# State space input matrices turned by VectorE blocks and DMA; fourth u lot one K tile later; last h_lo tiles ahead of the last u tiles

## The chip, the core and the metric

The kernel runs on one core of a Trainium2 chip. The metric is the device time of one launch in microseconds (us), the median of several runs; lower is better. The engines named here are TensorE (PE; its weight loads are PEld), VectorE (DVE), ScalarE (ACT), GpSimd (POOL) and SyncE (SP). SP computes nothing: it issues all DMAs of the kernel, in the order of its program, to one hardware queue that the core's 16 DMA engines serve.

## What is computed

The reference is a decoder trunk of two layers, for 512 tokens of 1024 channels in float32. Only the state space (S5) branch of the mixing part is touched by the change. There are 32 groups of 16 channels with 64 complex states each.

```
for l in range(DEPTH):                                   # DEPTH = 2
    x = x + 0.5 * swiglu(rms_norm(x, ffn1_norm[l]), ffn1_w1[l], ffn1_w3[l], ffn1_w2[l])
    h = rms_norm(x, mix_norm[l])
    p = h @ w_in[l]
    p_m2, p_s5, p_dsa, p_hg = jnp.split(p, IN_SPLITS, axis=-1)
    y_b = s5_branch(p_s5, ...)                           # beside mamba2, dsa and hgrn2 branches
    ...                                                  # gated merge, w_out
    x = x + 0.5 * swiglu(rms_norm(x, ffn2_norm[l]), ffn2_w1[l], ffn2_w3[l], ffn2_w2[l])

def s5_branch(u, ...):
    bb_re = q_re[..., None] * b_re - q_im[..., None] * b_im
    bb_im = q_re[..., None] * b_im + q_im[..., None] * b_re
    bu_re = jnp.einsum("blgi,gpi->blgp", ug, bb_re)      # the input matrices at work
    bu_im = jnp.einsum("blgi,gpi->blgp", ug, bb_im)
    _, _, s_re, s_im = lax.associative_scan(combine, (a_re, a_im, bu_re, bu_im), axis=1)
    y = einsum(s_re, c_re) - einsum(s_im, c_im) + d_skip * u ; y = gelu(y) ; GLU
```

## The kernel before

**Lots.** Every large product is cut into lots. A lot is one weight tile of 1024 x 128 (512 KB); its product with 512 tokens fills one PSUM bank. SP loads it into one of four slots of `raw`; ACT copies it to `w_hi` (L424), DVE or POOL forms `w_lo = raw - w_hi` (L432), and PE makes three passes for each of the eight K tiles (L493 to L495: hi by hi, lo by hi, hi by lo). A slot of `raw` is loaded anew when its `w_lo` is done. The order of the lots and of all other work in the mixing part is a list of steps, `script()`, that each engine walks in the same order. PE waits for `lo_done` of the lot and for its bank at `begin`, and for `h_done` of each K tile where the activations are fresh.

**The stage of the change.** The first feed-forward part ends with eight "down" lots. The mixing part begins with `s5_w` phase 0, then `quad` of u: four lots `u0` to `u3` of the state space input, walked K tile by K tile for all four, on activations that are not normalised yet. In between PE sums the squares (L536), ACT and DVE make `rstd`, and DVE writes the normalised tiles `normed`, which ACT copies over `h_hi` and DVE over `h_lo` (L1857) as soon as `quad` is through with a tile. DVE then scales the four u outputs into `s5_uc` (`keep_u`, L1863, shown in the trace as `s_uc`) and forms `w_lo` of the next lot. After `quad` come `s5_w` phase 1, the lots `ks` and `q0`, a small transpose `turn_small` (L720), `q1`, `q2`, and `s5_in` (L760): 128 matmuls for the 32 groups, stationary operand `s5_w`, moving operand `s5_u`. Lots `q3`, `k0` and then `s5_out` follow.

**The input matrices.** POOL computes them early, during the feed-forward part, as `s5_pre` (the trace writes `s_pre`, and so for all s5 names), with the 64 states of two groups on the partitions. `s5_in` needs them turned. `s5_w` does that on PE: eight times four transposes of 128x128 (L748) in two phases of 16 each, with eight copies from PSUM by ACT (L1531).

**SP's order in this stage**, all in one queue: `s5_taps` out to DRAM (8 DMAs, L1165), the lots up to `k`'s first ones, eight DMAs that load `s5_t` from `s5_taps` (L1171; 256 KB each, into 16 partitions each), four that store `s5_uc` to `s5_ud` in DRAM (L1177; 256 KB each, from 128 partitions, each after its `keep_u`), and, when all four have landed, two lots and eight DMAs that load `s5_u` (L1184; 128 KB each, into 16 partitions each). `s5_in` on PE waits for all eight of `s5_u`.

Of the kernel before, what the change touches and what calls it, by code (L numbers as in the profile page):

```python
# [20 lines left out]
S5_W_TURNS = ((0, 1, 2, 3), (4, 5, 6, 7))  # L21
S5_W_BANK = (4, 5, 6, 7, 4, 5, 6, 7)
# [25 lines left out]
def script():  # L48
# [33 lines left out]
    s = [("s5_w", 0), ("quad", "u", 0), ("s5_w", 1)] + lots(("ks", 1)) + [("lot", "q", 0), ("turn_small",)]  # L82
# [119 lines left out]
def trunk(nc, x_in, positions, w_lots, par_in, s5_in, con_in, gamma_in, out, s5_taps, s5_ud):  # L202
# [5 lines left out]
    with ctx:  # L208
# [35 lines left out]
        def PC(name, i):  # L244
# [26 lines left out]
        s5_pre = at("s5_pre", [P, 2, 16, P], f32, A + 13)  # L271
# [14 lines left out]
        s5_w = at("s5_w", [P, 2, 16, P], f32, M)  # L286
# [69 lines left out]
            s5_aj s5_ca_ready s5_mag_ready s5_gen s5_tap_psum s5_tap_done s5_tap_d s5_tap_out s5_w_psum s5_w_done  # L356
# [112 lines left out]
        def _(pe):  # L469
# [200 lines left out]
            def quad(kind, i):  # L670
# [66 lines left out]
            def s5_w_(phase):  # L737

                if phase == 0:
                    pe.wait_ge(S["s5_gen"], 1)  # L740
                for j in S5_W_TURNS[phase]:
                    if j == 6:

                        pe.wait_ge(S["rstd_ready"], R(2))
                    if j >= 4:
                        pe.wait_ge(S["s5_w_done"], j - 3)
                    for i in range(4):
                        m = pe.transpose(bank[S5_W_BANK[j]][:, P * i:P * (i + 1)], s5_pre[:, j // 4, 4 * (j % 4) + i],  # L748
                                         ident)
                    m.then_inc(S["s5_w_psum"], 1)  # L750
# [314 lines left out]
            def hg_end(h):  # L1065
# [4 lines left out]
                         quad=quad, s5_w=s5_w_, s5_in=s5_in_, s5_out=s5_out, s5_back=s5_back,  # L1070
# [25 lines left out]
        def _(sp):  # L1096
# [29 lines left out]
            for layer in range(DEPTH):  # L1126
# [171 lines left out]
        def _(act):  # L1298
# [146 lines left out]
            def lot(kind, i):  # L1445
# [9 lines left out]
                elif kind in ("q", "k"):  # L1455
                    evac(da_qk[:, 4 * "qk".index(kind) + i], n)
# [1135 lines left out]
```

## Time and profile before

| | |
|---|---|
| median of 3 runs | 2833.62 us (2833.0 to 2834.78) |
| profiled execution, from first to last instruction | 2830.9 us |
| PE busy | 2819.4 us of it |
| DVE, ACT, POOL busy | 1591.8, 1193.4, 708.1 us |
| DMA | 275.72 MB, mean 97 GB/s |
| instructions | 38776 |

The profiled execution's only own time is its span, 2830.9 us; it leaves out what lies before the first and behind the last instruction, and the median of the runs is 2.7 us more. An edit is priced in the span and the same number of microseconds is added to the median.

How to read it: PE is busy practically all the time, so a microsecond is won only where PE has less to do or waits less, and it is lost where PE begins to wait. Matmuls are pipelined, so the distance between the starts of two PE rows, not the length that a row states, is what a pass costs. The views used are the page's first part, the timeline of an engine (a row is a start, a length and what ran), the view of DMA issues with the time from issue to landing, and the view of stretches with the DMA rate in each.

### The profile page before, as it was taken

To read this page: it belongs to the slowest core of one execution; us is meant where nothing else is said; L and a number is where in the kernel's file an instruction comes from. 1 tells how busy PE (TensorE), PEld (TensorE's weight loads), DVE (VectorE), ACT (ScalarE), POOL (GpSimd) and SP (SyncE) were. 2 spreads that over 40 slices of the span, in tenths; PEclk is the share of its full clock that TensorE was granted. 3 is DMA by queue.
4 is the path that set the end of the run, shared out by engine and by line. 5 is a ranking of instruction groups with operands and counts; after the bars stand their busy time and mean duration, and the time that the engine had idled before them with its cause. 6 is when DMAs were issued, how large, how long until landed. Compare 5 with 4: busy or idle time off the path is not lost.

```text
span 2830.9 us, 38776 instructions
## 1 busy us (share of the span) xinstructions
PE 2819.4 (100%) x14364; PEld 2305.9 (81%) x14364; DVE 1591.8 (56%) x2312; ACT 1193.4 (42%) x1732; POOL 708.1 (25%) x336
## 2 busy tenths in 40 slices
PE   9999999999999999999999999999999999999999
PEld 7888888877788888888888888888777888888887
DVE  5575557685657454343544845576846673543433
ACT  5343354556355344222343423445553653442222
POOL 0075014333334440000000840234333344300000
PEclk9999999999999999999999999999999999999999
DMA  5333394222222233333333333932222223233332
GB/s 188 97 96 97 99 147 120 82 75 67 82 82 83 90 97 98 97 96 97 96 127 97 94 97 113 151 97 83 74 75 82 83 82 90 90 103 97 97 97 82
DMA packets 95601, 275.72 MB, mean 97 GB/s; under 512 B 17648, under 2 KB 30832, under 8 KB 94960
## 3 DMA queue, kind: packets, MB, share of 16 engines
q1 hardware_dynamic: 95472, 273.95, 34.2%
q8 instruction: 87, 1.43, 0.2%
q14 instruction: 42, 0.34, 0.0%
HBM read 264.48 MB, written 5.24 MB: 95 GB/s over the span
## 4 chain that ended last, share of the span: by engine, by line
PE 97%; DVE 2%; DMA 0%; ACT 0%; issue 0%; SPq 0%; ACTq 0%; DVEq 0%
PE bank L493 29%; PE bank L495 29%; PE bank L494 29%; PE bank L521 1%; PE bank L523 1%; PE bank L522 1%; PE bank L852 1%; PE bank L871 1%; PE bank L886 1%; PE bank L985 1%; PE bank L826 0%; DVE h_lo L1857 0%; PE bank L1043 0%; DVE s_uc L1863 0%; PE bank L1055 0%; PE bank L760 0%
## 5 line engine op out<-in xcount | busy, mean ns | idle before, releaser
L493 PE MATMUL bank<-h_hi,w_hi 128*128 128x512 f32 x2512 | 989.5, 394 | 2.4 <-DVE h_lo L1857 2.3
L495 PE MATMUL bank<-h_hi,w_lo 128*128 128x512 f32 x2512 | 978.1, 389 | 0.0
L494 PE MATMUL bank<-h_lo,w_hi 128*128 128x512 f32 x2512 | 977.8, 389 | 0.0
L424 ACT ACTIVATE w_hi<-raw 128x1024 fp32r<-128x1024 f32 x482 | 508.0, 1058 | 897.8 <-PE bank L495 881.5
L432 POOL TENSOR_TENSOR w_lo<-raw,w_hi 128x1024 fp32r<-128x1024 f32 x208 | 521.3, 2511 | 1090.5 <-ACT w_hi L424 1090.5
L493 PEld LDWEIGHTS bank<-h_hi,w_hi 128*128 128x128 f32 x2512 | 471.6, 188 | 108.2 <-issue 8.3
L495 PEld LDWEIGHTS bank<-h_hi,w_lo 128*128 128x128 f32 x2512 | 471.6, 188 | 99.2
L494 PEld LDWEIGHTS bank<-h_lo,w_hi 128*128 128x128 f32 x2512 | 471.8, 188 | 96.9 <-issue 1.9
L432 DVE TENSOR_TENSOR w_lo<-raw,w_hi 128x1024 fp32r<-128x1024 f32 x274 | 361.8, 1321 | 271.2 <-ACT w_hi L424 271.0
L493 PE MATMUL bank<-g_hi,w_hi 128*128 128x512 f32 x698 | 272.5, 390 | 0.0
L495 PE MATMUL bank<-g_hi,w_lo 128*128 128x512 f32 x698 | 271.6, 389 | 0.0
L494 PE MATMUL bank<-g_lo,w_hi 128*128 128x512 f32 x698 | 271.6, 389 | 0.0
L1892 DVE TENSOR_TENSOR gated<-bank,rstd 128x512 f32<-128x512 f32 x88 | 60.8, 691 | 217.0 <-PE bank L495 217.0
L1243 POOL TENSOR_TENSOR s_mag<-s_k,con 128x1024 f32<-128x1024 f32 x2 | 3.8, 1908 | 661.2 <-DVE s_k L2044 661.2
L1889 DVE TENSOR_TENSOR silu_a<-bank,rstd 128x512 f32<-128x512 f32 x88 | 60.7, 690 | 168.8 <-PE bank L495 147.3
L493 PEld LDWEIGHTS bank<-g_hi,w_hi 128*128 128x128 f32 x698 | 131.0, 188 | 28.4 <-DVE g_lo L1898 1.4
L495 PEld LDWEIGHTS bank<-g_hi,w_lo 128*128 128x128 f32 x698 | 131.0, 188 | 27.2
L494 PEld LDWEIGHTS bank<-g_lo,w_hi 128*128 128x128 f32 x698 | 131.1, 188 | 27.0
L493 PE MATMUL bank<-y_hi,w_hi 128*128 128x512 f32 x256 | 101.5, 396 | 0.0
L495 PE MATMUL bank<-y_hi,w_lo 128*128 128x512 f32 x256 | 99.8, 390 | 0.0
L494 PE MATMUL bank<-y_lo,w_hi 128*128 128x512 f32 x256 | 99.7, 389 | 0.0
L1502 ACT ACTIVATE gate_th<-bank 128x512 f32<-128x512 f32 x64 | 38.0, 594 | 140.4 <-PE bank L495 140.3
(374 smaller groups left out, 3336.9 us busy)
## 6 DMA issues: line engine op xcount, KB each, us to landing
raw<-in_w_lots SPq DMA_DIRECT2D x482, 512.0 KB, 3.6
s_t<-s_taps SPq DMA_DIRECT2D x16, 256.0 KB, 14.1
da_s<-da_qk SPq DMA_DIRECT2D x16, 256.0 KB, 4.1
x_nat<-in_x SPq DMA_DIRECT2D x4, 512.0 KB, 7.5
s_ud<-s_uc SPq DMA_DIRECT2D x8, 256.0 KB, 4.4
s_u<-s_ud SPq DMA_DIRECT2D x16, 128.0 KB, 8.8
s_bc<-in_s SPq DMA_DIRECT2D x2, 512.0 KB, 5.6
s_bp<-in_s SPq DMA_DIRECT2D x2, 512.0 KB, 6.6
```

The costliest lines, as they stand in the source:

```text
L424: act.activation(w_hi[:, s], raw[:, s], AFT.Copy).then_inc(S["hi_done"], 1)
L432: eng.tensor_tensor(w_lo[:, s], raw[:, s], w_hi[:, s].bitcast(f32), SUB).then_inc(S["lo_done"], 1)
L493: pe.matmul(b[:, :], w_hi[:, s, kw], xh[:, k], start=(k == 0), stop=False)
L494: pe.matmul(b[:, :], w_hi[:, s, kw], xl[:, k], start=False, stop=False)
L495: return pe.matmul(b[:, :], w_lo[:, s, kw], xh[:, k], start=False, stop=(k == nk - 1))
L521: pe.matmul(o, h_hi[:, k, tok], wh[:, :, k], start=(k == 0), stop=False)
L522: pe.matmul(o, h_lo[:, k, tok], wh[:, :, k], start=False, stop=False)
L523: m = pe.matmul(o, h_hi[:, k, tok], wl[:, :, k], start=False, stop=(k == KT - 1))
L852: m = pe.matmul(logit_bank(u, e)[:, 0:P * (b + 1)], da_qk[r, hp, P * b:P * (b + 1)], da_qk[r, 4 + hp, 0:P * (b + 1)], start=True, stop=True)
L1502: act.activation(gate_th[:, i % 2], bank[t % 4][:, :], AFT.Tanh, scale=0.5).then_inc(S["free%d" % (t % 4)], 1)
L1889: V.tensor_tensor(silu_a[:, q], bank[ta % 4][:, :], rstd[:, :], MUL).then_inc(S["free%d" % (ta % 4)], 1)
L1892: V.tensor_tensor(gated[:, q], bank[tb % 4][:, :], rstd[:, :], MUL).then_inc(S["free%d" % (tb % 4)], 1)
```

## The change

1. `s5_w` is taken out of the script on PE and ACT: 32 transposes and eight copies a layer, and the waits for them.
2. POOL writes the same numbers into `s5_pre` in another layout, in 24 instructions of 512 elements as before; the innermost elements that it writes now lie 64 bytes apart.
3. DVE turns `s5_pre` in place in blocks of 32x32 with two instructions, behind the down lots of the second third of the feed-forward part, and waits for `s5_gen` (POOL's end) before them.
4. SP stores the result to a new DRAM buffer `s5_wd` (2 DMAs of 1 MB, ahead of `s5_taps`) and loads it from there into `s5_w` (8 DMAs of 256 KB, into 32 partitions each) right behind the eight of `s5_t` and ahead of the four of `s5_uc`.
5. `s5_in` waits for these eight instead of ACT's copies, and reads `s5_w` with a distance of 64 bytes between neighbouring columns.
6. In `quad` the lot `u3` begins with K tile 1, and does its tiles 0 and 1 there; the first `h_step` is given there.
7. DVE writes the last two `h_lo` tiles before `keep_u(2)` and `keep_u(3)`, not after them.
8. ACT waits for `s5_w_out` before it writes `q0`'s output, which lies over `s5_pre`.

On SP, the place in layer 0 behind the first feed-forward part, before:

```order
L1134 DMA raw<-in_w_lots 128x1024
L1130 REGISTER_ALU
L1130 COMPARE_AND_BRANCH
L1171 DMA s_t<-s_taps 16x32x128 x8
L1177 DMA s_ud<-s_uc 128x512 x4
L1102 DMA raw<-in_w_lots 128x1024
L1184 DMA s_u<-s_ud 16x32x64 x4
L1102 DMA raw<-in_w_lots 128x1024
L1184 DMA s_u<-s_ud 16x32x64 x4
```

The same place of the changed kernel:

```order
L1118 DMA raw<-in_w_lots 128x1024
L1114 REGISTER_ALU
L1114 COMPARE_AND_BRANCH
L1158 DMA s_t<-s_taps 16x32x128 x8
L1164 DMA s_w<-s_wd 32x4x512 x8
L1169 DMA s_ud<-s_uc 128x512 x4
L1086 DMA raw<-in_w_lots 128x1024
L1176 DMA s_u<-s_ud 16x32x64 x4
L1086 DMA raw<-in_w_lots 128x1024
L1176 DMA s_u<-s_ud 16x32x64 x4
```

Eight DMAs, 2 MB in all, stand between `s5_t` and the stores of `s5_uc`; the rest keeps its order.

On DVE, the end of `quad` in layer 0, before:

```order
L1868 SCALAR_TENSOR_TENSOR normed<-x,par,rstd 128x512
L1863 TENSOR_TENSOR s_uc<-bank,rstd 128x512 x2
L432 TENSOR_TENSOR w_lo<-raw,w_hi 128x1024
L1863 TENSOR_TENSOR s_uc<-bank,rstd 128x512 x2
L1857 TENSOR_TENSOR h_lo<-normed,h_hi 128x512 x2
```

The same place of the changed kernel:

```order
L1856 SCALAR_TENSOR_TENSOR normed<-x,par,rstd 128x512
L1851 TENSOR_TENSOR s_uc<-bank,rstd 128x512 x2
L430 TENSOR_TENSOR w_lo<-raw,w_hi 128x1024
L1845 TENSOR_TENSOR h_lo<-normed,h_hi 128x512 x2
L1851 TENSOR_TENSOR s_uc<-bank,rstd 128x512 x2
```

The last two tiles of `h_lo` have changed places with the last two of `s5_uc`.

The diff, cut to its core:

```diff
-    s = [("s5_w", 0), ("quad", "u", 0), ("s5_w", 1)] + lots(("ks", 1)) + [("lot", "q", 0), ("turn_small",)]
+    s = [("quad", "u", 0)] + lots(("ks", 1)) + [("lot", "q", 0), ("turn_small",)]
...
-        s5_pre = at("s5_pre", [P, 2, 16, P], f32, A + 13)
+        s5_pre = at("s5_pre", [P, 2, 4, 32, S5_TILES], f32, A + 13)
...
-        s5_w = at("s5_w", [P, 2, 16, P], f32, M)
+        s5_w = at("s5_w", [P, 2, P, S5_TILES], f32, M)
...
                 for k in range(KT - 2):
                     pe.wait_ge(S["h_done"], H(H_RAW[1] + k + 1))
-                    for j in range(4):
+                    for j in range(4 if k else 3):
                         if k == 0:
                             begin(n0 + j, 0, OUT[n0] + j)
+                        if (k, j) == (1, 3):
+                            begin(n0 + 3, 0, OUT[n0] + 3)
+                            part(3, 0).then_inc(S["h_step"], 1)
                         m = part(j, k)
-                    m.then_inc(S["h_step"], 1)
+                    if k:
+                        m.then_inc(S["h_step"], 1)
...
             def s5_in_():
                 pe.wait_ge(S["s5_u_in"], 16 * S5_Q)
-                pe.wait_ge(S["s5_w_done"], 8)
+                pe.wait_ge(S["s5_w_in"], 16 * 8)
...
-                                          s5_w[:, c, st, 64 * e:64 * e + 64], s5_u[:, 2 * st + e], start=True, stop=True)
+                                          s5_w[:, c, 64 * e:64 * e + 64, st], s5_u[:, 2 * st + e], start=True, stop=True)
...
                 ring(3, MIX0 // 4)
+                for i in range(2):
+                    sp.wait_ge(S["s5_w_turned"], i + 1)
+                    sp.dma_start(s5_wd[i], s5_pre[:, i].rearrange("p b q a -> p b (q a)")).then_inc(S["s5_w_out"], 16)
                 sp.wait_ge(S["s5_tap_d"], 4)
...
+                sp.wait_ge(S["s5_w_out"], 32)
+                for i in range(2):
+                    blocks = s5_wd[i].rearrange("(a r) b x -> b r a x", a=4)
+                    for b in range(4):
+                        sp.dma_start(s5_w[32 * b:32 * b + 32, i].rearrange("r (a q) t -> r a (q t)", a=4), blocks[b]).then_inc(S["s5_w_in"], 16)
                 turn = FFN2_0 // 4 + 3
...
-                for t in range(4):
-                    r = slice(4 * t, 4 * t + 4)
-                    shape = [P, 4, S5_Q, 16]
-                    ar, an = (s5_pw[:, i, r, S5_Q + 1:S5_POW].unsqueeze(3).broadcast_to(shape) for i in (1, 4))
-                    bre, bim = (s5_bb[:, i, r].unsqueeze(2).broadcast_to(shape) for i in range(2))
-                    pre = [s5_pre[:, i, r].rearrange("p a (s i) -> p a s i", i=16) for i in range(2)]
+                for b in range(4):
+                    shape = [P, 16, 2, 16]
+                    at_ = S5_Q + 1 + 2 * b
+                    ar, an = (s5_pw[:, i, :, at_:at_ + 2].unsqueeze(3).broadcast_to(shape) for i in (1, 4))
+                    bre, bim = (s5_bb[:, i].unsqueeze(2).broadcast_to(shape) for i in range(2))
+                    pre = [s5_pre[:, i, b].rearrange("p (s i) a -> p a s i", s=2) for i in range(2)]
...
+                    if (kind, i) == ("q", 0):
+                        act.wait_ge(S["s5_w_out"], 32)
...
                 split_lo(V, MIX0 + 4)
+                rest(KT - 2)
+                rest(KT - 1)
                 keep_u(2)
                 keep_u(3)
-                rest(KT - 2)
-                rest(KT - 1)
...
+                elif phase == 3:
+                    V.wait_ge(S["s5_gen"], 1)
+                    for i in range(2):
+                        both = s5_pre[:, i].rearrange("p b q a -> p b a q")
+                        V.transpose(both, both).then_inc(S["s5_w_turned"], 1)
```

## Rows read from the trace of the kernel before

**Rows 1.** The page, its first line and the first line of busy times.

```profile
span 2830.9 us, 38776 instructions
PE 2819.4 (100%) x14364; PEld 2305.9 (81%) x14364; DVE 1591.8 (56%) x2312; ACT 1193.4 (42%) x1732; POOL 708.1 (25%) x336
```

**Rows 2.** Timeline of PE: start us, length us, what, [idle before and releaser]; both layers.

```profile
374.98 1.91 PE L748 MATMUL bank<-con,s_pre 128*128 128x128 f32 x16
376.64 0.48 PE L493 MATMUL bank<-h_hi,w_hi 128*128 128x512 f32 x1
...
378.78 0.39 PE L493 MATMUL bank<-h_hi,w_hi 128*128 128x512 f32 x1
...
399.38 1.91 PE L748 MATMUL bank<-con,s_pre 128*128 128x128 f32 x16
...
407.21 0.50 PE L493 MATMUL bank<-h_hi,w_hi 128*128 128x512 f32 x1 [1.15 <-DVE h_lo L1857]
...
425.00 3.95 PE L760 MATMUL bank<-s_u,s_w 128*64 128x64 f32 x128
...
1830.60 3.95 PE L760 MATMUL bank<-s_u,s_w 128*64 128x64 f32 x128
```

**Rows 3.** Timeline of SP: when single DMAs of layers 0 and 1 were issued.

```profile
387.19 2.29 SPq L1171 DMA_DIRECT2D s_t<-s_taps  x1
...
401.65 0.32 SPq L1177 DMA_DIRECT2D s_ud<-s_uc  x1
...
412.96 1.25 SPq L1184 DMA_DIRECT2D s_u<-s_ud  x1
...
1817.46 1.31 SPq L1184 DMA_DIRECT2D s_u<-s_ud  x1
```

**Rows 4.** DMA issues: KB each, us from issue to landing, of those four DMAs.

```profile
s_t<-s_taps SPq DMA_DIRECT2D x1, 256.0 KB, 16.2
...
s_ud<-s_uc SPq DMA_DIRECT2D x1, 256.0 KB, 4.0
...
s_u<-s_ud SPq DMA_DIRECT2D x1, 128.0 KB, 10.2
...
s_u<-s_ud SPq DMA_DIRECT2D x1, 128.0 KB, 11.1
```

**Rows 5.** Stretches: PE, PEld, DVE, ACT, POOL busy, PE clock, DMA share, GB/s.

```profile
383.00:397.00 14.00, 14.00 (x63) 11.57 (x62) 10.39 (x15) 7.47 (x10) 0.00 (x0) 1.00 1.28 102
423.00:427.00 4.00, 4.00 (x78) 3.38 (x78) 0.00 (x0) 2.49 (x3) 1.59 (x1) 1.00 1.01 404
485.00:491.00 6.00, 5.99 (x28) 4.50 (x28) 5.46 (x7) 2.23 (x6) 2.27 (x1) 1.00 0.90 208
...
2830.00:2831.00 1.00, 0.00 (x0) 0.00 (x0) 0.00 (x0) 0.00 (x0) 0.00 (x0) 0.54 0.00 0
```

**Rows 6.** Timelines of DVE and ACT about the start of mixing, layer 0.

```profile
376.27 1.23 DVE L432 TENSOR_TENSOR w_lo<-raw,w_hi 128x1024 fp32r<-128x1024 f32 x1 [0.40 <-ACT w_hi L424]
...
398.33 1.21 DVE L432 TENSOR_TENSOR w_lo<-raw,w_hi 128x1024 fp32r<-128x1024 f32 x1
399.46 2.16 DVE L1863 TENSOR_TENSOR s_uc<-bank,rstd 128x512 f32<-128x512 f32 x2
401.52 5.63 DVE L1857 TENSOR_TENSOR h_lo<-normed,h_hi 128x512 fp32r<-128x512 f32 x2
...
398.95 1.32 ACT L1524 ACTIVATE h_hi<-normed 128x512 fp32r<-128x512 f32 x2 [2.40 <-PE bank L495]
```

**Rows 7.** Timelines of POOL, DVE and ACT, earlier in layer 0.

```profile
254.69 0.53 POOL L1265 MEMSET s_tap<- 128x512 f32 x1
...
282.45 0.69 DVE L1889 TENSOR_TENSOR silu_a<-bank,rstd 128x512 f32<-128x512 f32 x1 [4.70 <-PE bank L495]
...
362.93 1.06 ACT L424 ACTIVATE w_hi<-raw 128x1024 fp32r<-128x1024 f32 x1 [1.89 <-PE bank L495]
```

**Rows 8.** Timeline of PE: its last instructions of the span.

```profile
2827.40 0.44 PE L654 MATMUL bank<-con,x 128*128 128x128 f32 x2 [0.30 <-DVE x L1923]
```

More of the change, by code:

```diff
@@ L20 @@
 S5_POW = 2 * S5_Q + 1
-S5_W_TURNS = ((0, 1, 2, 3), (4, 5, 6, 7))
-S5_W_BANK = (4, 5, 6, 7, 4, 5, 6, 7)
 PI = math.pi
@@ L199, with trunk @@
 CON_OFF = 97 * TILE + 96
-def trunk(nc, x_in, positions, w_lots, par_in, s5_in, con_in, gamma_in, out, s5_taps, s5_ud):
+def trunk(nc, x_in, positions, w_lots, par_in, s5_in, con_in, gamma_in, out, s5_taps, s5_ud, s5_wd):
     f32, f32r, i32, u32 = mybir.dt.float32, mybir.dt.float32r, mybir.dt.int32, mybir.dt.uint32
@@ L355, in trunk @@
         MIXED = """normed_ready h_step mg_hi_done mg_done s5_in s5_step s5_args s5_powers s5_phase s5_rot
-            s5_aj s5_ca_ready s5_mag_ready s5_gen s5_tap_psum s5_tap_done s5_tap_d s5_tap_out s5_w_psum s5_w_done
+            s5_aj s5_ca_ready s5_mag_ready s5_gen s5_tap_psum s5_tap_done s5_tap_d s5_tap_out s5_w_turned s5_w_out s5_w_in
             s5_u_out s5_u_in s5_bu s5_bu_used s5_state s5_taps_in s5_y s5_y2_act s5_y2_dve s5_back s5_y_used m2_zs
@@ L532, in norm_sums @@
                 pe.wait_ge(S["sq_used"], KT * (R(r) + 1))
-                if r == 1:
-                    pe.wait_ge(S["s5_w_done"], len(S5_W_TURNS[0]))
                 pe.matmul(bank[6][:, :], ones, sq_sum[:, :], start=True, stop=True).then_inc(S["sq_sums"], 1)
@@ L735, in branch @@
                     gemm(n, 0, y_hi, y_lo, BT, k0=BT * half, t0=OUT[n] + half, ready=None if half else ready)
[L737 to L750, printed above, removed]
             def s5_in_():
                 pe.wait_ge(S["s5_u_in"], 16 * S5_Q)
-                pe.wait_ge(S["s5_w_done"], 8)
+                pe.wait_ge(S["s5_w_in"], 16 * 8)
                 pe.wait_ge(S["small_done"], 1)
@@ L1069, in _ @@
                          gate=gate, branch=branch, merge=merge, da_square=da_square,
-                         quad=quad, s5_w=s5_w_, s5_in=s5_in_, s5_out=s5_out, s5_back=s5_back,
+                         quad=quad, s5_in=s5_in_, s5_out=s5_out, s5_back=s5_back,
                          s5_end=s5_end, da_norm=da_norm, da_rope=da_rope, da_index=da_index, da_topk=da_topk, att_start=att_start,
@@ L1526, in quad @@
                     split_hi(act, n + 4 + j)
-            def s5_w_(phase):
-                for j in S5_W_TURNS[phase]:
-                    act.wait_ge(S["s5_w_psum"], j + 1)
-                    act.activation(s5_w[:, j // 4, 4 * (j % 4):4 * (j % 4) + 4].rearrange("p a b -> p (a b)"),
-                                   bank[S5_W_BANK[j]][:, :], AFT.Copy).then_inc(S["s5_w_done"], 1)
             def s5_in_():
@@ L1777, in _ @@
                          gate=gate, branch=branch, merge=merge, da_square=da_square,
-                         quad=quad, s5_w=s5_w_, s5_in=s5_in_, s5_out=s5_out, s5_back=s5_back,
+                         quad=quad, s5_in=s5_in_, s5_out=s5_out, s5_back=s5_back,
                          s5_end=s5_end, da_norm=da_norm, da_rope=da_rope, da_index=da_index, da_topk=da_topk, att_start=att_start,
@@ L2053, in quad @@
                 normalise_h()
-            def s5_w_(phase):
-                pass
             def s5_in_():
@@ L2400, in _ @@
                          gate=gate, branch=branch, merge=merge, da_square=da_square,
-                         quad=quad, s5_w=s5_w_, s5_in=s5_in_, s5_out=s5_out, s5_back=s5_back,
+                         quad=quad, s5_in=s5_in_, s5_out=s5_out, s5_back=s5_back,
                          s5_end=s5_end, da_norm=da_norm, da_rope=da_rope, da_index=da_index, da_topk=da_topk, att_start=att_start,
@@ L2588 @@
     args.append(nc.dram_tensor("s5_ud", (BW, S5_Q, S5_CH), _mybir.dt.float32, kind="Internal").ap())
+    args.append(nc.dram_tensor("s5_wd", (2, P, 4, 16 * 32), _mybir.dt.float32, kind="Internal").ap())
     trunk(nc, *args)
```

## Prediction

> **What bounds the kernel now.** Read the page's busy times first: PE is busy 2819.4 us of a span of 2830.9 us [rows 1]. Whatever takes work from PE can help, up to the next thing that PE then meets. So the second view is PE's timeline about the start of mixing, where the change lies. PE comes from the down lots, does 16 transposes from 374.98 to 376.64 (1.66 us), runs `quad`, does 16 more from 399.38, walks `ks` and has to wait 1.15 us for the last `h_lo` until 407.21, and reaches `s5_in` at 425.00 (layer 1: 1830.60) with no wait shown [rows 2]. The third view is what `s5_in` needs: the eight loads of `s5_u`. The last was issued at 412.96 and took 10.2 us to land, so it landed at 423.2; in layer 1, 1817.46 + 11.1 = 1828.6 [rows 3, 4]. PE came 1.8 and 2.0 us later than that. This is the whole slack of the DMA chain, and it is the number that decides here: the chain is as long as PE's own path, less two microseconds.
>
> Follow that chain back. The last `s5_t` load, issued at 387.19, landed at 403.4; the last store of `s5_uc`, issued at 401.65, landed at 405.7 [rows 3, 4]; only then does SP issue the `s5_u` loads. Between 383 and 397 us the DMA engines show a share of 1.28 at only 102 GB/s [rows 5]: they work through the `s5_t` loads, without a gap, in the order of issue. A load that waited 16.2 us to land when its siblings take 2.6 us each (256 KB at 102 GB/s) had a queue before it.
>
> **Part 1, PE work that goes.** Two phases of 16 transposes: 2 x 1.66 = 3.3 us a layer. The wait of 1.15 us for `h_lo` goes too, see part 2. Where `quad` starts earlier, `u3` would meet its `w_lo`: DVE forms it from 376.27 to 377.50 [rows 6]; three K tiles of the other lots take 378.78 - 376.64 = 2.14 us [rows 2], so `u3` would have begun at 377.1, and in the new order it begins at about 379.2. No wait. ACT's eight copies go as well, and ACT is not what PE waits for. PE alone would reach `s5_in` 4.2 to 4.5 us earlier a layer: `ks` will wait some 0.3 us for its `w_lo`, since that ended at 399.54 [rows 6] and moves forward with `quad` by 1.66 us to 397.9, while PE is through with `quad` at 399.38 - 1.66 = 397.7. So PE arrives at about 425.00 - 4.2 = 420.8.
>
> **Part 2, DVE's order.** The two `h_lo` tiles took 5.63 us, from 401.52, at the end of the chain [rows 6]. Now they stand before `keep_u(2)`, right behind ACT's `h_hi` (398.95 + 1.32 - 1.66 = 398.6 at the end), and end by 400 even at 0.7 us each. `keep_u(2)` and `(3)` took 2.16 us and ended at 401.62 [rows 6]; behind the two tiles they end near 401.5. So the stores of `s5_uc` can be issued no earlier than before: the gain in PE's path does not come to the DMA chain.
>
> **Part 3, the eight new loads.** They are issued behind `s5_t` and ahead of the stores of `s5_uc`, in the same queue, 8 x 256 KB = 2.1 MB. SP issues them early (before 397 it waits for `keep_u` anyway), but the engines are held by `s5_t` until 403.4, so they run after it. Their price is the rate. Loads into 16 partitions ran at 102 GB/s, the stretch 485 to 491, in which four copies into 32 partitions each ran, shows 208, and lots into 128 partitions 404 [rows 5]. The new loads go into 32 partitions each: 2.1 MB / 208 GB/s = 10.1 us. The bounds are 5.2 us (404) and 20.6 us (102); I take 10.1, since that row has the same count of partitions. So the four stores land about 10.1 us later, SP issues the `s5_u` loads 10.1 us later, and the last lands at 423.2 + 10.1 = 433.3. `s5_in` begins there instead of at 425.0: 8.3 us later. In layer 1 it is 1828.6 + 10.1 - 1830.6 = 8.1 us. PE waits 433.3 - 420.8 = 12.5 us. All of parts 1 and 2 is inside this wait: 4.2 us a layer saved in front of a later join are worth nothing.
>
> The Trainium skill, "SBUF — State Buffer", section on the DMA port swizzle, says that a transfer's rate follows the ports that its partitions reach: 16 partitions about 109 GB/s, 32 about 218, all 128 up to 436. By that figure the eight loads would be an estimated 9.6 us instead of 10.1. The trace agrees, with 102, 208 and 404 GB/s [rows 5].
>
> **Part 4, `s5_in` itself.** It takes 3.9 us now [rows 2]. Two things can lengthen it. After 12 us of idling PE's clock will be down: at the end of the span PE's last row begins at 2827.40, and in 2830 to 2831 the granted clock reads 0.54 [rows 8, 5]; half of 2.4 GHz is its lower level. A stage run wholly at that level would take 3.9 us more, one run wholly at the upper level nothing. And the stationary operand is now read at a distance of 64 bytes; no row shows such a read, nothing excludes that it costs nothing, and I bound it by 0 and another 3.9 us (each read twice as slow). Neither can be a gain, since the same 128 matmuls run at a clock and from a layout that are at best as good as before. Of 0 to 7.8 us I take 2.0 a layer, half a doubling, since the clock comes back while the stage runs.
>
> The same page, in its note on SBUF lines, says that consecutive accesses should fall in the same 16-byte line, and that each new line costs. Every column of `s5_w` is such a new line, so by that rule the strided read would cost, an estimate of up to one more doubling; no run here shows it yet.
>
> **Part 5, what is hidden.** DVE's two turns: 2048 elements a partition each, at 1.21 us for 1024 [rows 6] about 2.4 us each, 4.8 in all. DVE idled 4.70 us at just that place, until 282.45 [rows 7], and nobody waits for that `silu_a` within the next lots. Its new wait for POOL: POOL was done at 255.2, DVE gets there at 277.75; 22 us for 24 instructions, so each may be 0.9 us longer for its strided writes. If it were more, all of DVE's `w_lo` would queue behind that wait. The stores to `s5_wd`: 2.1 MB at 404 GB/s, 5.2 us in the queue, issued near 346, ahead of `s5_taps` and the lot whose `w_hi` ACT starts at 362.93 on a release by PE [rows 7]; four slots of `raw` cover it. ACT's wait for `s5_w_out` is long over.
>
> **Sum.** 8.3 + 8.1 + 2 x 2.0 = 20.4 us. The span goes from 2830.9 to 2851.3, the median of the runs from 2833.6 to 2854.
>
> **Rivals.**
> *Fast loads.* The new loads run at 404 GB/s, since they come from DRAM in pieces of 2 KB and the copies in that 208 GB/s row are between partitions. Then 5.2 us: 423.2 + 5.2 - 425.0 = 3.4, layer 1 3.2, with the clock at 1 each: 8.6, so 2842. For it: that source differs. Against it: the 16-partition loads come from DRAM too, and were at a quarter.
> *Strided weights are dear.* Rate as forecast, `s5_in` doubled twice over: 16.4 + 2 x 7.8 = 32, so 2866.
> *Not slower.* The queue is not serial: while `s5_t` holds only the ports of 16 partitions, packets of the new loads slip beside it, and they are in before 403. Then the `s5_u` loads land at 423.2 as before, PE arrives at 420.8 and waits 2.4 us: gains 1.8 + 2.0 = 3.8 us, so 2829.8. The point from which it decides is that slack: the new loads may cost the chain less than 1.8 us. For it: 102 GB/s is a quarter of what the engines can move. Against it: a store issued at 401.65 landed in 4.0 us, only after the last `s5_t` at 403.4, and a share of 1.28 leaves no engine free. To gain all of PE's 4.2 us a layer (2825) the `s5_uc` stores would have to come earlier, and `keep_u` does not let them.
>
> **Chances.** The forecast 0.60 (2848 to 2860), fast loads 0.13, strided weights 0.12, not slower 0.14 of which 0.03 faster by more than 0.2%, the rest 0.01. A difference of 0.2%, 5.7 us, is about what measuring this kernel can tell from no change. Faster 0.03, same 0.11, slower 0.86. The range runs from fast loads without any clock loss (2840) to the dear weights (2866).
>
> **What would show it.** In the profile of the changed kernel: no transposes of `s_pre` on PE; a wait of about 12 us of PE before `s5_in` in each layer, released by a DMA (`s_u`); `s_w` loads landing between 403 and 414 and `s_ud` behind them; no wait for `h_lo` in `ks`; a granted clock under 1 behind the stall. A PE wait under 3 us before `s5_in`, or `s_ud` landing at 406, would prove the queue argument wrong; a wait of 7 us, the rate; an `s5_in` of over 8 us, the weight read.

## The result, and the profile after

| | us |
|---|---|
| before, median of 5 runs (range) | 2833.78 (2833.0 to 2834.78) |
| after, median of 5 runs (range) | 2858.65 (2855.89 to 2860.54) |
| difference of the medians | +24.9 |
| ratio, with its 95% interval | 1.0088 [1.0077, 1.0099] |
| profiled execution, span: before, after | 2830.9, 2854.1 (+23.2) |

The forecast was 2854 us, in a range of 2840 to 2866. The changed kernel is slower, by somewhat more than forecast. The profiled execution of after is the quickest of its five (2855.89), and in it 23.2 of the 24.9 us can be followed.

The first view is the page of after: the first line, the busy times, and from the part on the chain the shares by engine.

```profile
span 2854.1 us, 38652 instructions
PE 2820.1 (99%) x14300; PEld 2306.7 (81%) x14300; DVE 1597.4 (56%) x2316; ACT 1185.3 (42%) x1716; POOL 712.2 (25%) x336
...
PE 95%; DMA 2%; DVE 1%; SPq 1%; ACT 0%; issue 0%; ACTq 0%; DVEq 0%
```

Against [rows 1], PE has 64 instructions fewer and is 0.7 us longer busy, though 6.6 us of transposes went. So some other work on PE became dearer, and the rest of the 23 us is time in which PE does nothing. The list of PE's waits, which gives the idle time in all, the count and the longest, has one large entry:

```profile
PE bank L744 <- DMA s_u<-s_ud: 25.2, 2, 13.6
```

Line 744 is `s5_in`, which begins only when a DMA into `s_u` has landed. PE's timeline in both layers (start, length, idle before and releaser) shows where these 25.2 us are, and what came behind them:

```profile
375.27 0.39 PE L491 MATMUL bank<-h_hi,w_hi 128*128 128x512 f32 x1
...
432.33 7.41 PE L744 MATMUL bank<-s_u,s_w 128*64 128x64 f32 x128 [11.56 <-DMA s_u<-s_ud]
439.66 0.50 PE L491 MATMUL bank<-h_hi,w_hi 128*128 128x512 f32 x1
...
1850.44 7.55 PE L744 MATMUL bank<-s_u,s_w 128*64 128x64 f32 x128 [13.64 <-DMA s_u<-s_ud]
1857.92 0.50 PE L491 MATMUL bank<-h_hi,w_hi 128*128 128x512 f32 x1
```

The same place in the kernel before, the first matmul behind `s5_in` in each layer:

```profile
428.88 0.50 PE L493 MATMUL bank<-h_hi,w_hi 128*128 128x512 f32 x1
...
1834.48 0.50 PE L493 MATMUL bank<-h_hi,w_hi 128*128 128x512 f32 x1
```

With [rows 2] this gives the whole account. After's down lots end 0.29 us later (375.27 against 374.98), which is taken off in the first layer.

| term | layer 0 | layer 1 | sum |
|---|---|---|---|
| `s5_in` begins later | 432.33 - 425.00 - 0.29 = 7.0 | (1850.44 - 1830.60) - (439.66 - 428.88) = 9.1 | 16.1 |
| `s5_in` itself is longer, to the first matmul behind it | (439.66 - 432.33) - (428.88 - 425.00) = 3.45 | (1857.92 - 1850.44) - (1834.48 - 1830.60) = 3.6 | 7.05 |
| sum | 10.5 | 12.7 | 23.2 |

The sum is the difference of the spans. PE arrives at `s5_in` at 432.33 - 11.56 = 420.8 us: the gain of parts 1 and 2 is there, and lies whole inside the wait.

The queue is seen in SP's timeline (when a DMA was issued) and, for the same DMAs in the same order, in the list of issues (us from issue to landing). They are the last `s_t`, the last `s_w`, the last `s_ud` and the last `s_u` of layer 0:

```profile
387.78 2.41 SPq L1158 DMA_DIRECT2D s_t<-s_taps  x1
397.00 0.56 SPq L1164 DMA_DIRECT2D s_w<-s_wd  x1
401.75 0.77 SPq L1169 DMA_DIRECT2D s_ud<-s_uc  x1
422.06 1.23 SPq L1176 DMA_DIRECT2D s_u<-s_ud  x1
```

```profile
s_t<-s_taps SPq DMA_DIRECT2D x1, 256.0 KB, 14.9
...
s_w<-s_wd SPq DMA_DIRECT2D x1, 256.0 KB, 15.2
...
s_ud<-s_uc SPq DMA_DIRECT2D x1, 256.0 KB, 12.9
...
s_u<-s_ud SPq DMA_DIRECT2D x1, 128.0 KB, 10.2
```

Landings: 402.7, 412.2, 414.6, 432.3. The eight new loads are the 9.5 us between the first two; 2.1 MB in that time are 221 GB/s. The last store of `s5_uc` was issued at the same time as before [rows 3] but took 12.9 us instead of 4.0 [rows 4], since it stood behind them. PE begins `s5_in` at the very moment of the last landing.

### The profile page after: what moved, and what is told of

Same layout as the page of the kernel before. It is cut to its first block, busy times and chain, and to the rows that moved or that the text cites. A ratio compares the mean times of both kernels' runs of the same rounds, so it can differ in the third digit from the quotient of the medians.

```text
span 2854.1 us, 38652 instructions
## 1 busy us (share of the span) xinstructions
PE 2820.1 (99%) x14300; PEld 2306.7 (81%) x14300; DVE 1597.4 (56%) x2316; ACT 1185.3 (42%) x1716; POOL 712.2 (25%) x336
## 4 chain that ended last, share of the span: by engine, by line
PE 95%; DMA 2%; DVE 1%; SPq 1%; ACT 0%; issue 0%; ACTq 0%; DVEq 0%
PE bank L491 28%; PE bank L493 28%; PE bank L492 28%; PE bank L519 1%; PE bank L521 1%; PE bank L520 1%; DMA s_ud<-s_uc 1%; PE bank L836 1%; PE bank L855 1%; PE bank L870 1%; DMA s_u<-s_ud 1%; PE bank L969 1%; PE bank L744 1%; PE bank L810 0%; SPq L1176 0%; PE bank L1027 0%
```

## Experiments

Every ratio is against the kernel before, run beside it on the same chip; there before had medians of 2833.1 to 2833.2. Two theories of the 23 us stood against each other at first. The queue: the new loads hold the DMA engines for their own 9 to 10 us, so without them `s5_in` begins on time. Its rival: the loads slip beside the `s5_t` loads, and it is something else that delays the `s5_u` burst. A second question was the longer `s5_in`: the low clock behind the wait, or the read at 64 bytes' distance.

### The eight loads away

After, in which the eight loads are left out and DVE fills `s5_w` with zeros.

```diff
-                for i in range(2):
-                    blocks = s5_wd[i].rearrange("(a r) b x -> b r a x", a=4)
-                    for b in range(4):
-                        sp.dma_start(s5_w[32 * b:32 * b + 32, i].rearrange("r (a q) t -> r a (q t)", a=4), blocks[b]).then_inc(S["s5_w_in"], 16)
...
+                V.memset(s5_w[:, :, :, :].rearrange("p c q t -> p (c q t)"), 0.0).then_inc(S["s5_w_in"], 1)
```

> The changed kernel without its eight loads of s5_w; VectorE sets s5_w to zero at the start of mixing instead, in time in which it idles, so s5_in works on zeros (part of the computation is left out). Theory (one serial queue): s_ud lands at about 405.7 again, the last s_u at about 423.4, PE waits some 2.3 us before s5_in in each layer instead of 11.6 and 13.6. s5_in still reads with a distance of 64 bytes and takes 6.4 us at the upper clock. Time 2833.8 - 3.8 + 2 x 2.5 = 2835. Rival (the loads slip beside s5_t, and the time went elsewhere, into GpSimd's layout or VectorE's turns): PE still waits over 8 us, 2850 to 2859.

Measured: 2839.67 us, ratio 1.0021 [1.0012, 1.003]. PE's timeline at `s5_in`, both layers:

```profile
425.31 7.64 PE L744 MATMUL bank<-s_u,s_w 128*64 128x64 f32 x128 [4.76 <-DMA s_u<-s_ud]
...
1831.89 7.67 PE L744 MATMUL bank<-s_u,s_w 128*64 128x64 f32 x128 [2.11 <-DMA s_u<-s_ud]
```

The time above before falls from 24.9 us to 6.5, and `s5_in` of layer 0 begins at 425.31, 0.3 us from where it began before. The waits of 11.56 and 13.64 us have become 4.76 and 2.11. The rival is refuted. `s5_in` itself stays 3.7 us longer in each layer, where the expectation had 2.5. The wait of layer 0 is longer than expected too: the last `s_u` landed at 425.3 where [rows 3, 4] give 423.2 for before. The last `s_t` had landed 1.2 us later and the last `s_ud` 1.4 us later, although the same DMAs stood right ahead of them. Why is not shown; in the runs here whose eight `s5_t` loads go first, the last of them landed anywhere from 402.1 to 404.7. Both are why the time came out above the expectation.

### Only the strided read

Before, with nothing changed but the layout of `s5_w`: ACT's copies write it so that the stationary operand is read at a distance of 64 bytes, as in after.

```diff
-        s5_w = at("s5_w", [P, 2, 16, P], f32, M)
+        s5_w = at("s5_w", [P, 2, P, S5_TILES], f32, M)
...
-                                          s5_w[:, c, st, 64 * e:64 * e + 64], s5_u[:, 2 * st + e], start=True, stop=True)
+                                          s5_w[:, c, 64 * e:64 * e + 64, st], s5_u[:, 2 * st + e], start=True, stop=True)
```

> The kernel before, with s5_w laid out as in the changed kernel: ScalarE's eight copies write at a distance of 64 bytes and s5_in reads so. PE does not stall and its clock is at the upper level. Theory A (the strided read costs 50 ns a matmul where a packed one costs 30): s5_in 6.4 us, time 2833.8 + 2 x 2.5 = 2838.8. Theory B (only the clock): s5_in 3.9 us, 2833.8. ScalarE's copies may be longer, which is hidden either way.

Measured: 2840.81 us, ratio 1.0025 [1.0015, 1.0036]. PE's timeline at `s5_in`, and the stretch within the first (columns as in [rows 5]: the third from the end is the granted clock):

```profile
425.71 7.39 PE L760 MATMUL bank<-s_u,s_w 128*64 128x64 f32 x128
...
1835.04 7.45 PE L760 MATMUL bank<-s_u,s_w 128*64 128x64 f32 x128 [0.25 <-DMA s_u<-s_ud]
```

```profile
427.00:429.00 2.00, 2.00 (x40) 2.00 (x40) 0.00 (x0) 1.56 (x3) 1.79 (x1) 1.00 0.94 375
```

No stall, a clock of 1.00, and still 7.4 us instead of 3.95: 58 ns a matmul instead of 31. The read costs 3.45 to 3.5 us a layer, 7 us in all, and the time rises by 7.6; `s5_in` of layer 0 also begins 0.7 us later (425.71 against 425.00). The expectation missed low.

### Only the low clock

After, in which `s5_in` reads `s5_w` as if it were packed (other columns than it should).

```diff
-                                          s5_w[:, c, 64 * e:64 * e + 64, st], s5_u[:, 2 * st + e], start=True, stop=True)
+                                          s5_w[:, c].rearrange("p q t -> p (q t)")[:, P * st + 64 * e:P * st + 64 * e + 64], s5_u[:, 2 * st + e], start=True, stop=True)
```

> The changed kernel, with s5_in reading neighbouring elements of s5_w instead of every sixteenth, at the same wait. It multiplies by the wrong columns, so the state space branch's result is not the one wanted; the amount of work is the same. Theory A (the strided read costs): s5_in falls from 7.4 us to 5.0 to 5.5, what is left above 3.9 being the clock after the stall; time 2858.7 - 4.4 = 2854. Theory B (the clock alone costs): s5_in stays at 7.4 us and the time at 2858.7.

Measured: 2853.53 us, ratio 1.0068 [1.0053, 1.0083]. PE's timeline, and the stretches at the start of the stage and behind its fall in length:

```profile
433.93 6.00 PE L744 MATMUL bank<-s_u,s_w 128*64 128x64 f32 x128 [13.30 <-DMA s_u<-s_ud]
...
1850.94 5.79 PE L744 MATMUL bank<-s_u,s_w 128*64 128x64 f32 x128 [13.94 <-DMA s_u<-s_ud]
```

```profile
434.00:436.00 2.00, 2.00 (x38) 2.00 (x40) 0.00 (x0) 1.13 (x2) 0.00 (x0) 0.50 1.02 408
438.60:439.60 1.00, 1.00 (x42) 1.00 (x40) 0.00 (x0) 0.00 (x0) 1.00 (x1) 1.00 0.41 37
```

Here the clock does count: 20 matmuls a microsecond at 0.50 (1.2 GHz), 42 at 1.00 (2.4 GHz), and 1.8 to 2.05 us more than 3.95 for the stage. In after itself the same views read:

```profile
426.00:432.00 6.00, 0.00 (x0) 0.00 (x0) 0.00 (x0) 1.64 (x3) 2.34 (x1) 0.50 1.30 145
434.00:436.00 2.00, 2.00 (x40) 2.00 (x40) 0.00 (x0) 1.89 (x3) 1.46 (x1) 0.65 0.99 393
436.00:438.00 2.00, 2.00 (x40) 2.00 (x40) 0.00 (x0) 0.00 (x0) 2.00 (x2) 1.00 0.26 51
```

The clock fell in the wait and was back to 1.00 from 436 on. PE did 20 matmuls a microsecond both at 0.65 and at 1.00, and 30 in the 1.6 us from 432.4 to 434 at 0.50. So the two costs don't add. The four cases of `s5_in`:

| length of `s5_in`, us | no long wait before it (clock 1.00) | behind the wait of 12 to 14 us |
|---|---|---|
| packed read | 3.95 | 5.8 to 6.0 |
| read at 64 bytes' distance | 7.4 to 7.45 | 7.4 to 7.55 |

### Only DVE's order

Before, with the last two `h_lo` tiles ahead of `keep_u(2)` and `keep_u(3)`.

```diff
-                keep_u(2)
-                keep_u(3)
                 rest(KT - 2)
                 rest(KT - 1)
+                keep_u(2)
+                keep_u(3)
```

> The kernel before, with only VectorE's order changed: the last two h_lo tiles ahead of keep_u(2) and keep_u(3). PE's wait of 1.15 us for h_lo in ks goes. Theory (two chains of nearly equal length): the s_uc stores are issued 1.4 us later for it, so the last s_u lands at 424.6 and PE, there at 423.85, waits 0.8 us: gain 0.3 to 0.4 us a layer, 2833.1. Rival (the DMA chain has room): gain 1.15 us a layer, 2831.5, and no wait before s5_in.

Measured: 2832.35 us, ratio 0.9998 [0.9989, 1.0007]. DVE's timeline, and PE's at `s5_in`:

```profile
399.62 1.38 DVE L1857 TENSOR_TENSOR h_lo<-normed,h_hi 128x512 fp32r<-128x512 f32 x2
400.92 2.27 DVE L1863 TENSOR_TENSOR s_uc<-bank,rstd 128x512 f32<-128x512 f32 x2
```

```profile
423.56 3.95 PE L760 MATMUL bank<-s_u,s_w 128*64 128x64 f32 x128
...
1829.09 3.95 PE L760 MATMUL bank<-s_u,s_w 128*64 128x64 f32 x128 [1.37 <-DMA s_u<-s_ud]
```

The two tiles take 1.38 us and not 5.63 [rows 6], because they now run before POOL begins a `w_lo` beside them: POOL's first starts at 401.4 in both kernels. PE comes to `s5_in` 1.4 us earlier in layer 0; in layer 1 the wait of 1.37 us shows that it has met the end of the DMA chain. The theory held in layer 1 and its rival in layer 0. A gain of 1.5 us is in the trace (1829.09 against 1830.60), and the times can't tell it from nothing.

### The same loads, four times as wide

After, with the two halves of `s5_w` stored so that each comes back as one load of 1 MB into 128 partitions. The stores, four for each half instead of one, put the blocks in their place.

```diff
-                    sp.dma_start(s5_wd[i], s5_pre[:, i].rearrange("p b q a -> p b (q a)")).then_inc(S["s5_w_out"], 16)
+                    rows = s5_wd[i].rearrange("(b r) a x -> a r b x", b=4)
+                    for a in range(4):
+                        sp.dma_start(rows[a], s5_pre[32 * a:32 * a + 32, i].rearrange("p b q a -> p b (q a)")) \
+                          .then_inc(S["s5_w_out"], 16)
...
-                    for b in range(4):
-                        sp.dma_start(s5_w[32 * b:32 * b + 32, i].rearrange("r (a q) t -> r a (q t)", a=4), blocks[b]).then_inc(S["s5_w_in"], 16)
+                    sp.dma_start(s5_w[:, i].rearrange("p q t -> p (q t)"), s5_wd[i].rearrange("p a x -> p (a x)")) \
+                      .then_inc(S["s5_w_in"], 16)
```

> The changed kernel, with the load of s5_w as two DMAs of 1 MB into all 128 partitions; the stores to s5_wd are eight into the places that this needs. Same bytes, same place in the queue. Theory (the rate follows the count of partitions that a load writes): the loads take 5.2 us instead of 9.4 to 9.9, the last s_u lands 4.5 us earlier in each layer, time 2858.7 - 9 = 2850. Rival (the rate is that of reading pieces of 2 KB from DRAM): no change, 2858.7.

Measured: 2849.71 us, ratio 1.0053 [1.0038, 1.0068]. The stretches in which the loads ran, of this kernel and of after (the last column is GB/s):

```profile
405.00:409.00 4.00, 4.00 (x19) 3.32 (x18) 0.00 (x0) 0.88 (x2) 2.23 (x1) 1.00 0.98 406
```

```profile
405.00:412.00 7.00, 7.00 (x35) 5.54 (x34) 0.00 (x0) 0.70 (x2) 2.04 (x1) 1.00 1.06 241
```

After's stretch takes in the last microsecond, which the stores of `s5_uc` share; up to 411 it shows 218 GB/s. The same 2.1 MB ran in 4.7 us (from 404.7, when the last `s_t` had landed, to 409.4) instead of 9.5; in layer 1 they took 5.8 us instead of 9.0. The waits before `s5_in` fell to 9.20 and 11.09 us, 4.9 us in all where the expectation had 9. In layer 0 the `s_t` loads themselves landed 2.0 us later, and in each layer the `s_u` burst was 0.5 us longer, for reasons that weren't tried apart. The medians differ by 8.9, but this kernel has four runs and its profile is the slowest of them (2851.09), while that of after is its quickest; the trace decides the rate, and not how much of the time it brings.

### The loads ahead, half of the taps behind

After, with the eight `s_w` loads ahead of the `s_t` loads, and four of the eight `s_t` loads moved behind the `s5_u` loads, which `s5_in` doesn't need.

```diff
+                load_taps(0, 4)
...
-                for n in (2, 3):
-                    lot_after(next_lot + n)
+                lot_after(next_lot + 2)
+                load_taps(4, S5_Q)
+                lot_after(next_lot + 3)
```

> The changed kernel with SP's order changed alone: the eight s5_w loads first, then four of the eight s5_t loads; the other four follow behind the s5_u loads and one lot. Theory (only the bytes ahead of s_ud in the queue count): the queue ahead of s_ud is then 10 + 10 us, as long as the eight s5_t loads of the kernel before; s_ud lands near 405.7, the last s_u near 423.3, PE waits 2 to 4 us, s5_in takes 7.5 us: 2839, as without the loads (2839.7). s5_out, 11 us behind s5_in, would wait if its last s5_t lands after 441. Rival (any 2 MB more in this stage costs, wherever they stand): 2850 or more.

Measured: 2840.99 us, ratio 1.0025 [1.0015, 1.0035]. PE's timeline, and the last `s_ud` in SP's timeline and in the list of issues:

```profile
423.73 7.55 PE L744 MATMUL bank<-s_u,s_w 128*64 128x64 f32 x128 [3.14 <-DMA s_u<-s_ud]
```

```profile
401.55 0.32 SPq L1171 DMA_DIRECT2D s_ud<-s_uc  x1
```

```profile
s_ud<-s_uc SPq DMA_DIRECT2D x1, 256.0 KB, 3.1
```

The new loads are all still there, and the store of `s5_uc` lands in 3.1 us again. So it isn't what the loads do to memory or to PE that costs; it is their place in the queue. The time is now that of the strided read alone (2840.81). That is in part a coincidence: PE waits 7.1 us at `s5_in` in both layers together, less than it has saved, but it also waits 3.2 us in `s5_out` for DVE's `s_s`, a wait that neither before nor after has and that wasn't followed further.

### A packed `s5_w`, with early, wide loads

The kernel with the wide loads, but `s_wd` is loaded back much earlier, into the place of `s5_pre` (its values are in DRAM by then), and four copies by ACT and four by DVE write `s5_w` packed.

```diff
+        s5_wt = at("s5_wt", [P, 2, P, S5_TILES], f32, A + 13)
...
+                copy(s5_w[:, c, t], s5_wt[:, c, :, t].rearrange("p m t -> p t m")).then_inc(S["s5_w_packed"], 1)
...
-                ring(MIX0 // 4, MIX0 // 4 + 2)
+                ring(MIX0 // 4, MIX0 // 4 + 1)
+                sp.wait_ge(S["s5_w_out"], 128)
+                for i in range(2):
+                    sp.dma_start(s5_wt[:, i].rearrange("p q t -> p (q t)"), s5_wd[i].rearrange("p a x -> p (a x)")) \
+                      .then_inc(S["s5_w_in"], 16)
+                ring(MIX0 // 4 + 1, MIX0 // 4 + 2)
```

> The changed kernel, with the two wide loads moved ahead of the feed-forward part's end: they write over s5_pre, whose contents are in DRAM by then, four lots before mixing begins. ScalarE and VectorE then copy, in four pieces each and while they wait for the sums of squares, to a packed s5_w. Theory: no load of s5_w is left in the queue of s_ud, and s5_in reads neighbouring elements. The last s_u lands near 423.3, PE is there at 420.8 and waits 2.3 us, s5_in takes 3.95 us: gain 1.8 us a layer, 2830.2. Rival (the copies hold up the rstd chain or the early loads hold up the last lots): PE waits in quad or earlier, 2834 or more.

Measured: 2834.07 us, ratio 0.9999 [0.999, 1.0008]: equal to before, where a gain of 3 us was expected. PE's timeline at `s5_in` and a stretch within the first:

```profile
424.42 6.62 PE L753 MATMUL bank<-s_u,s_w 128*64 128x64 f32 x128 [3.67 <-DMA s_u<-s_ud]
...
1831.86 6.10 PE L753 MATMUL bank<-s_u,s_w 128*64 128x64 f32 x128 [4.21 <-DMA s_u<-s_ud]
```

```profile
424.50:427.00 2.50, 2.50 (x48) 2.50 (x50) 0.00 (x0) 1.48 (x3) 0.35 (x1) 0.50 1.03 411
```

Two things differ from the expectation. The last `s_u` of layer 0 landed 1.1 us later than the 423.3 it gave, so the waits are 3.7 and 4.2 us and not 2.3; what delayed it isn't shown. And the clock fell to 0.50 within each wait, so that the stage takes 6.6 and 6.1 us instead of 3.95. In this profile, which is the slowest of the eleven runs (2835.76; the quickest took 2829.12), what PE saved ahead of the join was almost all spent waiting, and cost 2.7 and 2.15 us more behind it.

### One lot of the burst ahead of the join

To that, the first of the two weight lots that are loaded among the `s5_u` loads moves ahead, between the second and the third store of `s5_uc`, where SP waits anyway.

```diff
                 for i in range(4):
 
+                    if i == 2:
+                        lot_after(MIX0 // 4 * 4 + 8)
...
                 for t in range(S5_Q):
-                    if t % 4 == 0:
-                        lot_after(next_lot + t // 4)
+                    if t == 4:
+                        lot_after(next_lot + 1)
```

> As the one before, and the first lot of the s5_u burst is loaded between the second and the third store of s5_uc, not behind the fourth. Theory (the s_u burst is a serial queue): 0.5 MB, 1.3 us, less stand between s_ud and the last s_u; it lands near 422.0, PE waits 1 us or less; gain 3 us a layer, 2827.8. Rival (the lot then delays s_ud by as much): 2830.2.

Measured: 2824.15 us, ratio 0.9969 [0.9958, 0.9979]: faster than before and after, and by more than was expected. The same kernel again, on another chip:

> The packed version with the lot ahead once more, to stand beside the next two on the same chip: 2824.2 again, within 1.5 us.

Measured: 2827.64 us, ratio 0.9976 [0.9966, 0.9985]. PE's timeline at `s5_in` of layer 1 in the first profile (2828.26 us) and in the second (2825.41 us), each with a stretch within it:

```profile
1824.43 5.50 PE L753 MATMUL bank<-s_u,s_w 128*64 128x64 f32 x128 [2.48 <-DMA s_u<-s_ud]
```

```profile
1824.50:1826.50 2.00, 2.00 (x42) 2.00 (x44) 0.00 (x0) 0.82 (x1) 0.00 (x0) 0.53 1.03 410
```

```profile
1823.42 3.95 PE L753 MATMUL bank<-s_u,s_w 128*64 128x64 f32 x128 [2.52 <-DMA s_u<-s_ud]
```

```profile
1823.50:1825.50 2.00, 2.00 (x70) 2.00 (x72) 0.00 (x0) 0.76 (x1) 0.00 (x0) 1.00 1.02 406
```

Two waits of equal length, 2.48 and 2.52 us; behind the one the clock is at 0.53 and the stage takes 5.50 us, behind the other at 1.00 and it takes 3.95. Of this kernel's 18 single times six lie between 2823 and 2824 and nine between 2827.4 and 2829.2, three between these groups. The clock of this one stage explains 1.55 of the 2.85 us between the two profiles. Another 1.0 us lies in layer 0: in the first profile PE, there at 420.45, waits 1.04 us for the last `s_u`, and in the second it comes at 420.40 and doesn't wait. So when the DMA chain ends varies by about a microsecond between executions of the same kernel, and the second expectation (within 1.5 us) gave too narrow a range.

### What of this is due to the change

Before, with DVE's order of the change and the same lot ahead, but `s5_w` still turned on PE:

> The kernel before (turns on PE), with VectorE's new order and with the first lot of the s5_u burst loaded between the second and the third s5_uc store. Theory (both chains must shorten together): PE comes to s5_in 1.15 us earlier, the last s5_u load about 1.3 us earlier than with the order alone, so PE does not wait: gain 1.15 us a layer, 2831.0 (the order alone gave 2832.4, no change that could be told). Rival (the queue is not what the order alone met): 2832.4 again.

Measured: 2829.8 us, ratio 0.9987 [0.9978, 0.9996]; no wait of PE at `s5_in` in either layer. So 3.4 us are to be had without turning anything by DMA, where the best kernel gains 5.6 on this chip (2827.64). The intervals can't tell the 2.2 us between them from none; that of the best kernel's first run ([0.9958, 0.9979], on another chip) just touches this one.

The best kernel without the later start of the fourth `u` lot:

```diff
-                    for j in range(4 if k else 3):
+                    for j in range(4):
...
-                        if (k, j) == (1, 3):
...
```

> As the packed version with the lot ahead, but u3 begins with K tile 0 as in the kernel before. Theory: PE, now 1.66 us earlier, waits about 0.6 us for u3's w_lo in quad; rstd and all behind it come 0.6 us later, PE reaches s5_in 0.6 us later, where it waits 1 to 2.5 us anyway, and the s5_uc stores come 0.6 us later: 0.6 us a layer, 2825.4. Rival (the later start of u3 does nothing): 2824.2 and no wait for w_lo.

Measured: 2825.61 us, ratio 0.9975 [0.9965, 0.9985]. PE's timeline at the fourth lot's first matmul, and at `s5_in` of layer 0:

```profile
377.41 0.50 PE L500 MATMUL bank<-h_hi,w_hi 128*128 128x512 f32 x1 [0.37 <-DVE w_lo L431]
...
423.79 5.50 PE L748 MATMUL bank<-s_u,s_w 128*64 128x64 f32 x128 [2.80 <-DMA s_u<-s_ud]
```

PE waits 0.37 us for its `w_lo`, so the delay by one K tile does what the prediction says of it. The times can't tell the two kernels apart: whatever PE saves there can be given back at `s5_in`, where this profile shows a stage of 5.50 us after a wait of 2.80.

The best kernel with DVE's old order:

```diff
-                rest(KT - 2)
-                rest(KT - 1)
                 keep_u(2)
                 keep_u(3)
+                rest(KT - 2)
+                rest(KT - 1)
```

> As the packed version with the lot ahead, but with VectorE's old order, keep_u(2) and keep_u(3) ahead of the last two h_lo tiles. Theory (the tiles then run beside GpSimd's w_lo and take 5 us, not 1.4): PE waits 3 to 3.5 us for h_lo in ks and comes to s5_in at 424, without a further wait there; s5_in stays at 3.95 us in both layers: 2 x 2.6 us more in start, 1.5 us less in s5_in, 2828. Rival (the order doesn't matter, since the DMA chain ends later anyway): 2824.2.

Measured: 2830.48 us, ratio 0.9986 [0.9977, 0.9995]. PE's timeline, layer 0, and DVE's:

```profile
402.92 0.50 PE L500 MATMUL bank<-h_hi,w_hi 128*128 128x512 f32 x1 [0.43 <-DVE h_lo L1861]
...
405.68 0.50 PE L500 MATMUL bank<-h_hi,w_hi 128*128 128x512 f32 x1 [1.80 <-DVE h_lo L1861]
```

```profile
400.10 5.53 DVE L1861 TENSOR_TENSOR h_lo<-normed,h_hi 128x512 fp32r<-128x512 f32 x2
```

Once PE is early, the old order makes it wait 2.2 us for `h_lo` in layer 0 (4.4 in all; 3 to 3.5 a layer were expected), and PE then finds no wait at `s5_in`, which takes 3.95 us in both layers. The medians on this chip differ by 2.8 us (2830.48 against 2827.64), but the intervals overlap, so the waits are shown and the gain in time is not. In after, which waits 12 to 14 us at `s5_in`, such a gain would lie inside the wait; this wasn't run.

## Why the prediction was right, point by point

**PE's path (parts 1 and 2)** held: PE arrives at 420.8, there is no wait of `ks` for `h_lo` and none of `u3` for `w_lo`. That it holds to the tenth is luck: the wait of 0.3 us of `ks` for its `w_lo` didn't come, and the stage began 0.29 us later. DVE ended its `s_uc` at 401.7 (forecast 401.5):

```profile
398.14 1.37 DVE L1845 TENSOR_TENSOR h_lo<-normed,h_hi 128x512 fp32r<-128x512 f32 x2
399.43 2.29 DVE L1851 TENSOR_TENSOR s_uc<-bank,rstd 128x512 f32<-128x512 f32 x2
```

The working is off in two places that cancel. The 0.7 us a tile that it took as a bound was the true length, and with it its own terms give 398.6 + 1.4 + 2.16 = 402.2, not 401.5; the two tiles began at 398.14, half a microsecond sooner.

**The queue (part 3)** was the right mechanism, and the experiments without the loads and with the loads ahead show it. The rate was taken from a row with the same count of partitions: 10.1 us against 9.5 in layer 0 (and 9.0 in layer 1, from 1819.6 to 1828.6). The start of `s5_in` was forecast 8.3 and 8.1 us later, and was 7.0 and 9.1. The sum is right (16.4, measured 16.1), in part by luck, since the parts are off both ways. In layer 0 the last store of `s5_uc` landed 9.0 us later and the last `s_u` 9.1. In layer 1, against a layer that begins 10.8 us later, the last `s_u` landed 11.0 us later: 9.0 are the loads, 1.2 the burst behind the stores (19.3 us from the first lot's issue at 1831.04, against 18.1 from 1810.47), 0.8 the `s_t` loads and stores. What that burst met wasn't tried apart. The fast-loads rival (404 GB/s for all DRAM sources) is refuted by the 221 GB/s; the same bytes ran at 406 only when they went into 128 partitions. The Trainium skill, "SBUF — State Buffer", Door 1: The DMA port swizzle, makes the rate depend on the ports that a transfer's partitions reach. The trace agrees at 102 [rows 5], 221 and 406 GB/s.

**`s5_in` itself (part 4)** is the term that was mis-sized: 2.0 us a layer, measured 3.45 and 3.6. It was taken as half a doubling, with the clock in mind as the cause of what would be lost. The runs show the reverse. The strided read alone costs 3.45 us with a clock of 1.00, the clock alone 1.8 to 2.05 us, and both together no more than the read alone. The bound of 7.8 us, which added them, was reached in no run. That is the 3 us by which the profiled execution exceeds the working: 20.4 + 3.05 (this term) - 0.3 (the start) = 23.2. The other 1.7 us to the medians' difference is the spread of after's runs, and isn't located. The Trainium skill, "SBUF — State Buffer", in its note on SBUF lines under Door 1, says that each access which crosses to a new 16-byte line pays a penalty. The trace agrees: 58 ns for a matmul with 64 such columns, 31 ns for one whose columns lie side by side. That the lines are the cause wasn't tried apart, since only the distance of 64 bytes was run.

**What was hidden (part 5)** stayed hidden, with less to spare than forecast. DVE's timeline at the turns and POOL's at the end of its work on `s_tap`:

```profile
277.98 7.53 DVE L2038 STREAM_TRANSPOSE s_pre<-s_pre 128x2048 f32<-128x2048 f32 x2
285.41 0.64 DVE L1877 TENSOR_TENSOR silu_a<-bank,rstd 128x512 f32<-128x512 f32 x1
```

```profile
258.57 0.53 POOL L1257 MEMSET s_tap<- 128x512 f32 x1
```

The turns took 7.53 us and not 4.8, which is more than the 4.70 us that DVE had idled there: `silu_a` came 3.0 us later than in [rows 7], and no wait of PE followed. POOL came to the memset behind its strided writes 3.9 us later, against 22 us of room.

**The rivals.** "Not slower" fell with the queue: the loads did not slip beside the `s5_t` loads. Strided weights are dear in fact, but by one doubling instead of two, and the time stayed under 2866. The signs named in the prediction came: waits of 11.6 and 13.6 us (forecast 12.5), `s_w` landing up to 412, `s_ud` behind it, and a granted clock of 0.50 in the wait.

## What to carry to other kernels

PE time saved ahead of a join is worth only the slack that the other branch leaves. Read the landing time of the last DMA at the join first, and follow its queue back: a load that goes in front of it costs the whole of bytes over rate, and the rate goes by the partitions it reaches. Then price what the wait does behind it (the clock), and what a new layout does to the engine that reads it. Where the bytes must be moved, what helped here was an early place in the queue, 128 partitions at once, and a packed copy made by engines that had time.

## What the runs showed of the hardware

- Where the stationary f32 operand of 64 columns is read at 64 bytes' distance, a matmul takes 58 ns instead of 31. At this read the lower clock adds almost nothing (30 matmuls in 1.6 us at 0.50, 20 a microsecond at 0.65 and at 1.00; the whole stage took 7.4 us at 1.00 and 7.4 to 7.7 behind waits).
- PE's granted clock fell to 0.50 within waits of 3.67 and 4.21 us. Behind waits of 2.11 (the run without the loads, layer 1), 2.48 and 2.80 us it went down to 0.50 while PE was already at work again; behind one of 2.52 us, and in those of 0.89 and 1.04 us, it stayed at 1.00. With the packed read this lost 1.55 to 2.7 us, so that such a wait of 2.5 to 4 us cost 1.5 to 1.7 times its length. Behind the waits of 13 to 14 us the loss was no larger, 1.8 to 2.05 us.
- DVE's two `h_lo` tiles take 1.4 us by themselves and 5.5 to 5.6 us next to a `w_lo` of POOL, so a DVE instruction's place can be worth more than its length.
- DVE's turn of 32x32 blocks in place over 2048 elements a partition took 3.77 us (7.53 for two), where 1024 elements of a subtraction take 1.21 [rows 6].
